# 512-column products, an opening in pieces, column groups in Compressed's first layer and operands at multiples of 512 bytes in a two-block, four-layer kernel

## The chip, the cores and the metric

One core of a Trainium2 chip runs the whole program. The metric is the device time of one execution in microseconds (us), shown as the median of the runs. The engines are PE (TensorE, which multiplies), DVE (VectorE), ACT (ScalarE), POOL (GpSimd) and SP (SyncE, which here issues every DMA).

## The reference, cut to what matters

The input is 256 tokens of width 1024, in float32. Two layers of a first block, then two layers of a second.

```python
# first block, each layer
x = x + 0.5 * (silu(a) * b) @ w2              # a, b = split(rms_norm(x) @ w1), D_FF = 2816
h = rms_norm(x); proj = h @ w_in
ys = gmlp(proj), retention(proj), nsa(proj)   # nsa has the compressed, selected and window branches
x = x + sum(sigmoid(h @ w_gate[b] + bias[b]) * (ys[b] @ w_branch[b]) for b in 3) @ w_o
x = x + 0.5 * swiglu_ffn(rms_norm(x))
# second block, each layer
u = rms_norm(x); proj = u @ w_in
ys = fourier(proj), gqa(proj), mlstm(proj), diff_attention(proj, rel_bias)
x = x + sum(sigmoid(gates[b]) * (ys[b] @ w_branch[b]) for b in 4) @ w_out
x = x + (gelu(conv3(a)) * lin) @ w_down       # a, lin = split(rms_norm(x) @ w_up)
```

Compressed is the branch of nsa that joins windows of 32 tokens into a vector and sends it through a two-layer net (`gelu(flat @ w1) @ w2`).

## The kernel before, in words

**Arithmetic.** Each weight and each activation is split into a high and a low part of type float32r, and a product of matrices is three passes: high by high, high by low, low by high (`three_passes`, L392). In a pass the first operand is stationary (128 x 128) and the second moves through, a column at a time.

**The ring.** All large weights come as 370 tiles of 128 x 2048 values (1 MB). `Ring` (L161) has five slots. For a tile, SP issues the load when the slot is used up (`loads_to`), ACT copies it into its high part (`hi_to`, L198), DVE subtracts to get the low part in place (`lo_to`, L206), and PE waits for that (`ready`). How far ahead each engine works is written out by hand: the calls of `hi_to` and `lo_to` stand between an engine's other work, and each engine runs its list in order.

**Two ways to multiply.** `features_major` (L402) has the weights stationary and hT (the normalised input, features on partitions) moving, 256 tokens wide; `tokens_major` (L413) has hT stationary and 256 weight columns moving. Either takes 48 products of 256 columns for a tile. Down tiles, the output projection and its equal in block two have 512 weight columns moving: 24 products for a tile.

**A feed-forward stage** (`Ffn`, L437) has 11 pairs of up tiles and 11 down tiles. The first pair is done by tokens, so that it can start when the first 128 tokens are normalised, and is turned afterwards (`turn`). Then PE takes up(i, 0), up(i, 1), down(i-1). The up tile fills one PSUM bank with the two halves a and b; ACT applies silu (L567), DVE multiplies by b (L615), ACT and DVE split the result g (L583, L619). In block two a convolution over tokens stands ahead (L572, L607, L610, L577).

**A middle stage** mixes. `Fill` (L670) is a list of units, the halves of projection, gate and branch tiles, which PE works through between the small products of the mixers (`f.tensor(pe, n)`); two PSUM banks take turns. A gate unit ends in a tanh on ACT (L800), a branch unit in one or two DVE operations (L819, L823). `Out` (L834) splits the mixed sum and multiplies it with the output projection.

**Joins.** Between two stages `Join` (L361) adds the result to x, takes the root mean square (ACT L264, POOL L271 to L276), scales (L317, L334), turns on PE (L353) and splits into hT_hi (ACT L325) and hT_lo (DVE L342), for each half of the tokens. PE does products of the first half while the second is being prepared.

**The opening** (`Start`, L2094) does the same for the input, loads the first tiles, and makes the table of relative-position biases: four products give 128 equal rows per head (L2130), DVE copies them (L2139), SP writes them to DRAM and loads them back with a shift of one per partition.

**Compressed** (L1099) has its first layer at L1236: for each of two nets 16 products with the weights stationary and 32 window columns moving.

**Places in SBUF.** Tensors follow each other without gaps, at multiples of 32 bytes. hT and the weight slots have one residue modulo 512 bytes; the overlay with the operands of the stages has others, among them g of the first block, g of the second, and the branch inputs.

```python
pe.matmul(out, w[0], x[0], start=start, stop=False)         # three_passes, L394 to L396
pe.matmul(out, w[0], x[1], start=False, stop=False)
return pe.matmul(out, w[1], x[0], start=False, stop=stop)
```

Of the kernel before, what the change touches and what calls it, by code (L numbers as in the profile page):

```python
# [14 lines left out]
P = 128  # L15
# [22 lines left out]
PROJ1_TILES = 16  # L38
F1_AT = 0
# [6 lines left out]
PROJ2_TILES = 20  # L46
PROJ2_AT = 0
# [76 lines left out]
class Core:  # L124


    def __init__(self, nc, ctx):
# [11 lines left out]
        self.ident = sb("ident", [P, P])  # L139
        self.neg_half = sb("neg_half", [P, 32])  # L140
        self.mean_sq, self.rstd = sb("x_mean_sq", [P, 2, NT, 2]), sb("x_rstd", [P, 2, NT])
# [5 lines left out]
        self.used = [sem(f"w_used{i}") for i in range(SLOTS)]  # L147
        self.res_ok, self.squared, self.rooted, self.xn_dve, self.xn_act, self.turned, self.hT_hi_ok, self.hT_lo_ok = (
# [11 lines left out]

class Ring:  # L161

# [11 lines left out]
    def close(self):  # L174
        self.slot = [n % SLOTS for n in range(len(self.places))]
        self.nth, self.before = [], []
        loads, count = [0] * SLOTS, [0] * SLOTS
        for j, s in zip(self.slot, self.signals):
            loads[j] += 1
            self.nth.append(loads[j])  # L180
            self.before.append(count[j])
            count[j] += s

    def loads_to(self, sp, n):
        for m in range(self.loaded, min(n, len(self.places))):
            slot, at = self.slot[m], self.places[m]
            if self.before[m]:
# [3 lines left out]
            self.loaded = m + 1  # L191

# [168 lines left out]
class Join:  # L361
# [14 lines left out]
    def vector(self, dve):  # L376
        for t in range(NT):
# [45 lines left out]

def ffn_places(base):
# [8 lines left out]
FFN_SIGNALS = [1] * (FFN_TILES - 1) + [2]  # L433
FFN_BYTES = 14336


class Ffn:  # L437
# [3 lines left out]
    def __init__(self, k, ph, r, at, n0, which, norm, conv, res):  # L441
# [6 lines left out]
                                  for j in range(2)] for i in range(2)] for n, a in (("hi", 6144), ("lo", 10240)))  # L448
        self.act_done, self.g_done, self.ghi_done, self.glo_done, self.mid_done, self.conv1, self.conv2 = (
# [7 lines left out]
        self.ab, self.ab0 = k.bank[0:2], k.bank[2:4]  # L457
# [9 lines left out]
    def up(self, pe, i, j):  # L467
# [3 lines left out]
        if i == 1:  # L471
            pe.wait_ge(self.first_ok[j], self.which + 1)
        else:
            pe.wait_ge(self.g_done[j], self.base + i)
        for half in range(2):
            last = features_major(pe, k, slot, half, self.ab[j][:, half * SEQ:(half + 1) * SEQ])
        last.then_inc(k.used[slot], 1)

    def first_up(self, pe, j, t):
        k, n = self.k, self.up_at(0, j)  # L480
        slot = k.ring.slot[n]
        k.ring.ready(pe, n)
        last = tokens_major(pe, k, slot, t, self.ab[j][:, t * 256:(t + 1) * 256],
                            (lambda c: self.norm.ready(pe, t, c)) if j == 0 else None)
# [53 lines left out]
    def scalar(self, act):  # L538
        k = self.k
        for j in range(2):  # L540
            k.ring.wait_used(act, self.up_at(0, j), 1)
            act.activation(self.first[j][:], self.ab[j][:].rearrange("p (t n) -> p t n", t=NT), ACT.Copy
                           ).then_inc(self.first_ok[j], 1)
            k.ring.hi_to(act, self.n0 + SLOTS - 1 + j)
        for j in range(2):
# [3 lines left out]
        for i in range(1, FFN_PAIRS):  # L549
            for j in range(2):  # L550
                self.activate(act, i, j)
                k.ring.hi_to(act, self.up_at(i, j) + SLOTS)
                self.split_hi(act, i, j)
            if i < FFN_PAIRS - 1:
                k.ring.hi_to(act, self.up_at(i, 1) + 1 + SLOTS)

    def activate(self, act, i, j):
        k, at = self.k, self.base + i
        if i:
            k.ring.wait_used(act, self.up_at(i, j), 1)  # L560
        else:
            act.wait_ge(self.first_mm[j], self.which + 1)
        a = self.ab[j] if i else self.ab0[j]
        if self.conv is None:
            if at:
                act.wait_ge(self.g_done[j], at)
            act.activation(self.s1[j][:], a[:, 0:SEQ], ACT.Silu).then_inc(self.act_done[j], 1)  # L567
# [2100 lines left out]
```

## Time and profile before

| | |
|---|---|
| median of 3 runs | 2402.84 us (2400.41 to 2406.5) |
| the profiled execution | 2401.82 us |
| its span, from the first to the last instruction | 2400.1 us |
| mean granted TensorE clock | 0.994 of 2.4 GHz |
| busy: PE, weight loads, DVE, ACT, POOL | 98%, 93%, 58%, 47%, 3% |
| read from HBM | 401.93 MB, 168 GB/s over the span |

The busy share of PE counts overlapping products once, and tells whether it has something to do, not how fast it does it. The distance between the starts of successive products, read from the timeline, tells that. A group of instructions is named by its line, engine and operation, then what it writes and reads (output, arrow, moving operand, stationary operand for PE).

### The profile page before, as it was taken

How to read it: one execution, taken by the hardware profiler on the slowest of the kernel's cores; microseconds unless marked ns; L12 is line 12 of the kernel's file. 1: busy time of each engine (PE TensorE's matmuls, PEld its weight loads, DVE VectorE, ACT ScalarE, POOL GpSimd, SP SyncE). 2: the span in 40 equal slices, each digit the busy share in tenths (PEclk: the TensorE clock that was granted, in tenths of full speed). 3: DMA queues.
4: the chain of work that ended last, by engine and by line, in shares of the span. 5: the costliest groups of instructions: out<-in, count | busy, mean ns of one | idle time of the engine just before them, and what ended most of it. 6: DMA issues, size and time to landing. Idle time of an engine off the chain costs nothing.

```text
span 2400.1 us, 40143 instructions
## 1 busy us (share of the span) xinstructions
PE 2363.1 (98%) x17520; PEld 2233.6 (93%) x17520; DVE 1391.8 (58%) x1730; ACT 1138.0 (47%) x1595; POOL 61.9 (3%) x110
## 2 busy tenths in 40 slices
PE   8999999999999999999999999999999999999998
PEld 7999999999999999999999899999999999999998
DVE  4446656654454466565544655686655655685665
ACT  5435445454354354454543544355545444355543
POOL 0000000000000000000000100000000100000000
PEclk9999999999999999999999999999999999999999
DMA  6564543455555545334555434344555434345553
GB/s 249 181 216 176 198 141 124 158 176 185 184 176 183 214 176 198 129 124 170 209 187 182 158 137 145 135 147 176 185 188 181 159 141 150 131 158 182 178 190 109
DMA packets 60254, 407.13 MB, mean 170 GB/s; under 512 B 7696, under 2 KB 9232, under 8 KB 12464
## 3 DMA queue, kind: packets, MB, share of 16 engines
q1 hardware_dynamic: 60080, 404.58, 47.2%
q8 instruction: 138, 2.26, 0.4%
q14 instruction: 36, 0.29, 0.0%
HBM read 401.93 MB, written 2.10 MB: 168 GB/s over the span
## 4 chain that ended last, share of the span: by engine, by line
PE 89%; DVE 4%; ACT 2%; DMA 2%; issue 1%; POOL 1%; SPq 0%; POOLq 0%; ACTq 0%; DVEq 0%
PE bank L394 27%; PE bank L396 27%; PE bank L395 27%; DVE w_lo L206 2%; DMA w_raw<-in_tiles 2%; DVE hT_lo L342 1%; PE bank L1236 1%; PE bank L1631 1%; PE bank L1458 1%; PE bank L1318 1%; POOL x_rstd L276 1%; PE bank L1855 0%; ACT w_hi L198 0%; ACT a_sq L264 0%; PE bank L1881 0%
## 5 line engine op out<-in xcount | busy, mean ns | idle before, releaser
L394 PE MATMUL bank<-hT_hi,w_hi 128*128 128x256 f32 x3408 | 973.3, 286 | 2.2 <-ACT b_dv L805 1.3
L395 PE MATMUL bank<-hT_lo,w_hi 128*128 128x256 f32 x3408 | 965.6, 283 | 0.0
L396 PE MATMUL bank<-hT_hi,w_lo 128*128 128x256 f32 x3408 | 965.5, 283 | 0.0
L206 DVE TENSOR_TENSOR w_lo<-w_raw,w_hi 128x2048 fp32r<-128x2048 f32 x370 | 843.0, 2285 | 129.9 <-ACT w_hi L198 129.6
L198 ACT ACTIVATE w_hi<-w_raw 128x2048 fp32r<-128x2048 f32 x370 | 705.5, 1909 | 192.2 <-DMA w_raw<-in_tiles 192.0
L394 PEld LDWEIGHTS bank<-hT_hi,w_hi 128*128 128x128 f32 x3408 | 654.3, 192 | 7.5 <-issue 1.9
L395 PEld LDWEIGHTS bank<-hT_lo,w_hi 128*128 128x128 f32 x3408 | 654.5, 192 | 2.6
L396 PEld LDWEIGHTS bank<-hT_hi,w_lo 128*128 128x128 f32 x3408 | 654.3, 192 | 0.0
L615 DVE TENSOR_TENSOR a_ffn_g<-a_ffn_act,bank 128x256 f32<-128x256 f32 x88 | 37.1, 421 | 339.5 <-ACT a_ffn_act L567 339.4
L394 PE MATMUL bank<-w_hi,hT_hi 128*128 128x256 f32 (+1 forms) x736 | 214.9, 292 | 12.3 <-DVE hT_lo L342 9.9
L396 PE MATMUL bank<-w_hi,hT_lo 128*128 128x256 f32 (+1 forms) x736 | 211.6, 287 | 0.0
L395 PE MATMUL bank<-w_lo,hT_hi 128*128 128x256 f32 (+1 forms) x736 | 211.5, 287 | 0.0
L567 ACT ACTIVATE a_ffn_act<-bank 128x256 f32<-128x256 f32 x88 | 33.8, 384 | 295.4 <-PE bank L396 283.9
L394 PEld LDWEIGHTS bank<-w_hi,hT_hi 128*128 128x128 f32 x736 | 145.4, 198 | 19.3 <-issue 10.3
L395 PEld LDWEIGHTS bank<-w_lo,hT_hi 128*128 128x128 f32 x736 | 145.8, 198 | 0.1
L396 PEld LDWEIGHTS bank<-w_hi,hT_lo 128*128 128x128 f32 x736 | 145.6, 198 | 0.0
L394 PE MATMUL bank<-w_hi,a_ffn_g_hi 128*128 128x512 f32 x352 | 140.2, 398 | 0.0
L395 PE MATMUL bank<-w_lo,a_ffn_g_hi 128*128 128x512 f32 x352 | 139.7, 397 | 0.0
L396 PE MATMUL bank<-w_hi,a_ffn_g_lo 128*128 128x512 f32 x352 | 139.7, 397 | 0.0
L607 DVE SCALAR_TENSOR_TENSOR b_ffn_conv<-bank,cols,b_ffn_conv 128x255 f32<-128x255 f32 x44 | 21.2, 482 | 107.1 <-ACT b_ffn_conv L572 107.0
L396 PEld LDWEIGHTS bank<-w_hi,a_ffn_g_lo 128*128 128x128 f32 x352 | 66.5, 189 | 16.2
L394 PEld LDWEIGHTS bank<-w_hi,a_ffn_g_hi 128*128 128x128 f32 x352 | 66.5, 189 | 14.1
(336 smaller groups left out, 2794.6 us busy)
## 6 DMA issues: line engine op xcount, KB each, us to landing
w_raw<-in_tiles SPq DMA_DIRECT2D x370, 1024.0 KB, 4.8
a_cmp_w<-in_cmp_w SPq DMA_DIRECT2D x2, 2048.0 KB, 8.1
a_gm_rows<-in_rows SPq DMA_DIRECT2D x2, 768.0 KB, 6.8
x_res<-in_x SPq DMA_DIRECT2D x2, 512.0 KB, 4.9
rel_line<-a_line SPq DMA_DIRECT2D x1, 1024.0 KB, 8.9
a_ret_rows<-in_rows SPq DMA_DIRECT2D x2, 512.0 KB, 8.4
b_rows<-in_rows SPq DMA_DIRECT2D x2, 512.0 KB, 6.8
out<-x_res SPq DMA_DIRECT2D x4, 256.0 KB, 2.0
```

The lines of the kernel that those rows point to most:

```text
L198: act.activation(k.hi[slot][:], k.raw[slot][:], ACT.Copy).then_inc(k.hi_done[slot], 1)
L206: dve.tensor_tensor(k.lo[slot][:], k.raw[slot][:], k.hi[slot][:].bitcast(F32), ALU.subtract).then_inc(k.lo_done[slot], 1)
L276: pool.tensor_tensor(out, out, k.neg_half[:, 0:1], ALU.pow).then_inc(k.rooted, 1)
L342: dve.scalar_tensor_tensor(out=k.hT_lo[:, c, ts], in0=self.turned(t, c), scalar=self.gain[:, c:c + 1], in1=k.hT_hi[:, c, ts].bitcast(F32), ...
L394: pe.matmul(out, w[0], x[0], start=start, stop=False)
L395: pe.matmul(out, w[0], x[1], start=False, stop=False)
L396: return pe.matmul(out, w[1], x[0], start=False, stop=stop)
L567: act.activation(self.s1[j][:], a[:, 0:SEQ], ACT.Silu).then_inc(self.act_done[j], 1)
L615: dve.tensor_tensor(self.g[j][:], self.s1[j][:], a[:, SEQ:2 * SEQ], ALU.mult).then_inc(self.g_done[j], 1)
L1236: last = pe.matmul(k.bank[i][:, 0:32], self.w1[:, i, j], self.win[i][:, j].rearrange("p g n -> p (g n)"), start=(j == 0), stop=(j == 15))
L1318: last = pe.transpose(k.bank[2 + u % 2][:, j * P:(j + 1) * P], pr[u % 2][:, j * P:(j + 1) * P], k.ident[:])
L1458: last = pe.matmul(self.out_bank[c][:, 0:SEQ], self.m[:, t, c, part * P:(part + 1) * P], self.dft_seq[:, t, part * SEQ:(part + 1) * SEQ], ...
```

## The change

- Up tiles: hT_hi and hT_lo lie next to each other for each group of 128 features. The high weights meet both in one product of 512 columns, the low weights meet hT_hi in one of 256 columns, written over the second half of the bank (`with_both`). A half of an up tile now fills a bank of its own with two partial sums, which ACT (`copy`) and DVE (`add_parts`) add up. The up tiles use four banks in place of two.
- Projections that come out by tokens, and the gates and branches of the second block, move 512 weight columns (`wide`, roles "wide", "wgate", "wbranch"); the weights are laid out on the host to fit (`tile_wide`). The mixed sum of block two is therefore by tokens, and `TurnedOut` turns it on PE ahead of the output projection.
- The first two weight tiles are loaded and split in quarters, and the order of the opening on ACT and DVE is another. The bias table is one product with four rows; the DMA to DRAM repeats them 128 times.
- In Compressed's first layer the windows are stationary and the weights move. Product j goes to the column group j mod 4, that is to 32 of PSUM's partitions; a closing product with four stacked unit matrices adds the groups.
- In a join and at the start of an FFN, weight splits on DVE stand at other places.
- x, hT, the weight slots and the operands of the stages start at multiples of 512 bytes.

The diff, cut to its core:

```diff
+WIDE1 = (0, 6, 8)
+WIDE2 = (0, 10, 12, 18)
...
@@ Core.__init__
+        self.ident = sb("ident", [P, P])
+        self.neg_half = sb("neg_half", [P, 32])
+        self.four, self.four_ok = sb("four", [P, 32]), ctx.enter_context(nc.semaphore("four_ok"))
+        self.mean_sq, self.rstd = sb("x_mean_sq", [P, 2, NT, 2]), sb("x_rstd", [P, 2, NT])
+        sb("up_to_2048", [P, (2048 - nc.sbuf_base) // 32 * 8])
         self.x = sb("x_res", [P, NT, D])
-        self.hT_hi = sb("hT_hi", [P, KC, SEQ], F32R)
-        self.hT_lo = sb("hT_lo", [P, KC, SEQ], F32R)
+        self.hT = sb("hT", [P, KC, 2, SEQ], F32R)
+        self.hT_hi, self.hT_lo = self.hT[:, :, 0], self.hT[:, :, 1]
...
@@ Ring (SPLIT = 2 tiles, PIECES = 4), loads_to and new helpers
+            if m < SPLIT:
+                for q in range(PIECES):
+                    src = self.tiles[at:at + 1, :, q * PIECE:(q + 1) * PIECE]
+                    sp.dma_start(self.piece(self.k.raw, m, q), src.rearrange("a p n -> (a p) n")
+                                 ).then_inc(self.k.piece_in[m][q], 16)
+                self.loaded = m + 1
+                continue
...
+    def piece_hi(self, act, m, q):
+        act.wait_ge(self.k.piece_in[m][q], 16)
+        act.activation(self.piece(self.k.hi, m, q), self.piece(self.k.raw, m, q), ACT.Copy).then_inc(self.k.piece_hi, 1)
...
+    def chunk_ready(self, pe, n, c):
+        if n >= SPLIT:
+            if c == 0:
+                self.ready(pe, n)
+        elif c % 2 == 0:
+            pe.wait_ge(self.k.piece_lo, PIECES * n + c // 2 + 1)
...
@@ Join.vector
                 self.norm.vector_xn(dve, t)
-                self.k.ring.lo_to(dve, self.end + 2 + t)
+                if t == 0:
+                    self.k.ring.lo_to(dve, self.end + 2)
                 self.norm.vector_lo(dve, t)
+        if self.norm is not None:
+            self.k.ring.lo_to(dve, self.end + 3)
...
+def wide(pe, k, slot, t, kh, out, ready=None):
+    ts = slice(t * P, (t + 1) * P)
+    for c in range(KC // 2):
+        at = kh * KC // 2 + c
+        if ready is not None:
+            ready(at)
+        w = slice(c * 512, (c + 1) * 512)
+        last = three_passes(pe, out, (k.hT_hi[:, at, ts], k.hT_lo[:, at, ts]), (k.hi[slot][:, w], k.lo[slot][:, w]),
+                            kh == 0 and c == 0, kh == 1 and c == KC // 2 - 1)
+    return last
+def with_both(pe, k, slot, half, bank):
+    for c in range(KC):
+        at = c * 256 + half * P
+        pe.matmul(bank[:], k.hi[slot][:, at:at + P], k.hT[:, c].rearrange("p a s -> p (a s)"), start=c == 0, stop=False)
+        last = pe.matmul(bank[:, SEQ:2 * SEQ], k.lo[slot][:, at:at + P], k.hT_hi[:, c], start=False, stop=c == KC - 1)
+    return last
...
@@ Ffn.up, from the second pair on
-            pe.wait_ge(self.g_done[j], self.base + i)
+        elif i > 1:
+            pe.wait_ge(self.summed[j], self.parts(i - 1, 1))
         for half in range(2):
-            last = features_major(pe, k, slot, half, self.ab[j][:, half * SEQ:(half + 1) * SEQ])
-        last.then_inc(k.used[slot], 1)
+            with_both(pe, k, slot, half, self.ab[j][half]).then_inc(k.used[slot], 1)
...
@@ Ffn.scalar
         for i in range(1, FFN_PAIRS):
             for j in range(2):
+                self.copy(act, i, j, 0)
+                if not (i == FFN_PAIRS - 1 and j):
+                    k.ring.hi_to(act, self.up_at(i, j) + SLOTS - 1)
                 self.activate(act, i, j)
-                k.ring.hi_to(act, self.up_at(i, j) + SLOTS)
+                self.copy(act, i, j, 1)
                 self.split_hi(act, i, j)
...
+    def copy(self, act, i, j, half):
+        k.ring.wait_used(act, self.up_at(i, j), half + 1)
+        act.activation((self.b if half else self.s1)[j][:], self.ab[j][half][:, SEQ:2 * SEQ], ACT.Copy
+                       ).then_inc(self.copied[j], 1)
...
@@ Ffn.vector (combine's convolution is now a function of its own, convolve)
-        ring.lo_to(dve, self.n0 + SLOTS - 1)
-        for j in range(2):
-            self.combine(dve, 0, j)
         ring.lo_to(dve, self.n0 + SLOTS)
         for j in range(2):
+            self.convolve(dve, 0, j)
+            self.combine(dve, 0, j)
+        for j in range(2):
             self.split_lo(dve, 0, j)
+        ring.lo_to(dve, self.n0 + SLOTS + 1)
         for i in range(1, FFN_PAIRS):
             for j in range(2):
+                self.add_parts(dve, i, j, 0)
+                ring.lo_to(dve, self.up_at(i, j) + SLOTS - 2)
+                self.convolve(dve, i, j)
+                self.add_parts(dve, i, j, 1)
                 self.combine(dve, i, j)
                 self.split_lo(dve, i, j)
+            ring.lo_to(dve, self.up_at(i, 1) + SLOTS - 1)
+    def add_parts(self, dve, i, j, half):
+        out = (self.b if half else self.s1)[j]
+        dve.wait_ge(self.copied[j], self.parts(i, half))
+        dve.tensor_tensor(out[:], self.ab[j][half][:, 0:SEQ], out[:], ALU.add).then_inc(self.summed[j], 1)
...
@@ Fill.product
+        if role[0] in ("wide", "wgate"):
+            ready = (lambda c: self.norm.ready(pe, half, c)) if n <= self.n0 + 1 else None
+            last = wide(pe, k, slot, half, role[-1], bank[:], ready)
...
+        elif role[0] == "wbranch":
+            ts = slice(half * P, (half + 1) * P)
+            for kc in range(YC):
+                w = slice(kc * BW, (kc + 1) * BW)
+                last = three_passes(pe, bank[:], (y_hi[:, kc, ts], y_lo[:, kc, ts]),
+                                    (k.hi[slot][:, w], k.lo[slot][:, w]), kc == 0, kc == YC - 1)
...
+class TurnedOut(Out):
+    def turn(self, pe, half):
+        k, f = self.k, self.f
+        pe.wait_ge(f.mixed, f.mix_at[self.ends[half] - 1])
+        if half:
+            pe.wait_ge(self.mlo_ok, 2)
+        for c in range(KC // 2):
+            for t in range(NT):
+                at, col = (c % 2) * SEQ + t * P, (KC // 2 * half + c) * P
+                last = pe.transpose(k.bank[4 + c // 2][:, at:at + P], f.mix[:, t, col:col + P], k.ident[:])
...
@@ Compressed.tensor
             for j in range(16):
-                last = pe.matmul(k.bank[i][:, 0:32], self.w1[:, i, j], self.win[i][:, j].rearrange("p g n -> p (g n)"),
-                                 start=(j == 0), stop=(j == 15))
-            last.then_inc(self.hid_mm, 1)
-        f.tensor(pe, 2)
+                q = slice(32 * (j % 4), 32 * (j % 4) + 32)
+                last = pe.matmul(k.bank[2 + i][q, 0:P], self.win[i][:, j].rearrange("p g n -> p (g n)"),
+                                 self.w1[:, i, j], start=(j < 4), stop=(j >= 12))
+            last.then_inc(self.part_mm, 1)
+        f.tensor(pe, 1)
+        pe.wait_ge(k.four_ok, 1)
+        for i in range(2):
+            pe.wait_ge(self.part_ok, i + 1)
+            pe.matmul(k.bank[i][:, 0:32], self.parts[i][:], k.four[:], start=True, stop=True).then_inc(self.hid_mm, 1)
+        f.tensor(pe, 1)
...
@@ Start
-        self.line = r.at("line", 39040, [P, DIFF_HEADS, self.W])
+        self.line = r.at("line", 8192, [DIFF_HEADS, self.W])
...
-        k.ring.loads_to(sp, 1)
+        k.ring.loads_to(sp, 2)
...
-        sp.wait_ge(self.copied, DIFF_HEADS)
-        sp.dma_start(line_dram.rearrange("h p n -> p h n"), self.line[:]).then_inc(self.line_out, 16)
+        sp.wait_ge(self.copied, 1)
+        sp.dma_start(line_dram.rearrange("h p n -> h p n"),
+                     self.line[:].unsqueeze(1).broadcast_to([DIFF_HEADS, P, self.W])).then_inc(self.line_out, 16)
...
-        for h in range(DIFF_HEADS):
-            pe.matmul(self.k.bank[4 + h][:], self.rel[:, h:h + 1].broadcast_to([32, P]), self.onehot[:], start=True,
-                      stop=True).then_inc(self.made, 1)
+        pe.matmul(self.k.bank[4][0:DIFF_HEADS, :], self.rel[:], self.onehot[:], start=True, stop=True
+                  ).then_inc(self.made, 1)
...
@@ program: regions of the overlay start at multiples of LINE
+LINE = 512
+        sb("up_to_a_line", [P, -nc.sbuf_base % LINE // 32 * 8])
-        p1.end = 15456
-        r1 = Region(p1, 47424)
+        p1.end = 31 * LINE
+        r1 = Region(p1, 93 * LINE)
-            first.append(Ffn(k, ffn, r1, 24704, a, 2 * l, norm, None, 0.5))
+            first.append(Ffn(k, ffn, r1, 24576, 39424, a, 2 * l, norm, None, 0.5))
+        p2.end = 31 * LINE
+        r2 = Region(p2, 73 * LINE)
...
+def tile_wide(w):
+    N = w.shape[1]
+    return w.reshape(2, KC // 2, P, N // 512, 512).transpose(3, 0, 2, 1, 4).reshape(N // 256, P, TILE)

```

## Rows read from the trace of the kernel before

**Rows 1.** The page: span; busy us, share, count; the chain that ended last, by engine.

```profile
span 2400.1 us, 40143 instructions
PE 2363.1 (98%) x17520; PEld 2233.6 (93%) x17520; DVE 1391.8 (58%) x1730; ACT 1138.0 (47%) x1595; POOL 61.9 (3%) x110
PE 89%; DVE 4%; ACT 2%; DMA 2%; issue 1%; POOL 1%; SPq 0%; POOLq 0%; ACTq 0%; DVEq 0%
```

**Rows 2.** TensorE timeline (start, length, us): up tile, then block-two branch tile.

```profile
106.33 0.28 PE L394 MATMUL bank<-hT_hi,w_hi 128*128 128x256 f32 x1
...
111.72 0.28 PE L394 MATMUL bank<-hT_hi,w_hi 128*128 128x256 f32 x1
...
1543.60 0.28 PE L394 MATMUL bank<-b_z_hi,w_hi 128*128 128x256 f32 x1
...
1546.24 0.28 PE L395 MATMUL bank<-b_z_lo,w_hi 128*128 128x256 f32 x1
```

**Rows 3.** Timeline of TensorE: down tiles of the first block, then of the second.

```profile
100.38 0.40 PE L394 MATMUL bank<-w_hi,a_ffn_g_hi 128*128 128x512 f32 x1
...
105.28 0.40 PE L394 MATMUL bank<-w_hi,a_ffn_g_hi 128*128 128x512 f32 x1
...
1700.69 0.40 PE L394 MATMUL bank<-w_hi,b_ffn_g_hi 128*128 128x512 f32 x1
...
1704.82 0.39 PE L394 MATMUL bank<-w_hi,b_ffn_g_hi 128*128 128x512 f32 x1
```

**Rows 4.** Timeline of TensorE in the opening, at half clock.

```profile
17.62 0.41 PE L395 MATMUL bank<-w_lo,hT_hi 128*128 128x256 f32 x1
17.83 0.41 PE L396 MATMUL bank<-w_hi,hT_lo 128*128 128x256 f32 x1
```

**Rows 5.** Groups by form, TensorE: shapes, count, then busy us, mean ns, idle.

```profile
L394 PE MATMUL bank<-w_hi,a_ffn_g_hi 128*128 128x512 f32 x352 | 140.2, 398 | 0.0
L1236 PE MATMUL bank<-a_cmp_win,a_cmp_w 128*128 128x32 f32 x128 | 14.6, 273 | 0.0
L1258 PE MATMUL bank<-a_cmp_kcT,a_nqT 64*128 64x32 f32 x64 | 4.0, 274 | 0.0
```

**Rows 6.** Groups by form, DVE and ACT.

```profile
L206 DVE TENSOR_TENSOR w_lo<-w_raw,w_hi 128x2048 fp32r<-128x2048 f32 x370 | 843.0, 2285 | 129.9 <-ACT w_hi L198 129.6
L615 DVE TENSOR_TENSOR a_ffn_g<-a_ffn_act,bank 128x256 f32<-128x256 f32 x88 | 37.1, 421 | 339.5 <-ACT a_ffn_act L567 339.4
L567 ACT ACTIVATE a_ffn_act<-bank 128x256 f32<-128x256 f32 x88 | 33.8, 384 | 295.4 <-PE bank L396 283.9 <-PE bank L492 11.3
```

**Rows 7.** Windows: busy us (count) of PE, PEld, DVE, ACT, POOL; PEclk, DMA, GB/s.

```profile
1683.00:1869.00 186.00, 184.18 (x1289) 171.72 (x1288) 113.01 (x133) 95.65 (x116) 0.98 (x3) 1.00 0.53 186
```

**Rows 8.** Timeline of a join, DVE and then TensorE.

```profile
220.61 2.27 DVE L206 TENSOR_TENSOR w_lo<-w_raw,w_hi 128x2048 fp32r<-128x2048 f32 x1
222.81 2.15 DVE L342 SCALAR_TENSOR_TENSOR hT_lo<-bank,cols,hT_hi 128x128 fp32r<-128x128 f32 x8
...
223.20 0.39 PE L394 MATMUL bank<-w_hi,hT_hi 128*128 128x256 f32 x1 [1.15 <-DVE hT_lo L342]
```

**Rows 9.** Timeline of TensorE in the opening.

```profile
6.35 7.19 PE L2130 MATMUL bank<-a_onehot,a_rel 32*128 32x512 f32 x8 [6.35 <-DMA a_onehot<-in_onehot]
...
17.27 0.55 PE L394 MATMUL bank<-w_hi,hT_hi 128*128 128x256 f32 x1 [0.52 <-DVE hT_lo L342]
...
30.86 0.36 PE L394 MATMUL bank<-w_hi,hT_hi 128*128 128x256 f32 x1 [0.54 <-DVE hT_lo L342]
```

**Rows 10.** DMA, first 60 us: GB/s by slice; issues, KB, us to landing.

```profile
GB/s 0 186 301 246 404 391 429 426 421 437 431 404 285 385 437 415 297 22 0 0 0 11 0 109 426 333 431 98 0 197 431 363 233 98 377 235 0 120 426 153
rel_line<-a_line SPq DMA_DIRECT2D x1, 1024.0 KB, 8.9
```

**Rows 11.** Timeline where the first convolution FFN starts, DVE and then TensorE.

```profile
1697.16 2.28 DVE L206 TENSOR_TENSOR w_lo<-w_raw,w_hi 128x2048 fp32r<-128x2048 f32 x1
...
1699.92 0.47 PE L394 MATMUL bank<-w_hi,b_ffn_g_hi 128*128 128x512 f32 x1 [1.23 <-DVE b_ffn_g_lo L619]
```

More of the change, by code:

```diff
@@ L704, in __init__ @@
         for u, (n, h, last, group, role) in enumerate(self.units):
-            if not last and role[0] not in ("gate", "branch"):
+            if self.partial(last, role):
                 continue
-            if role[0] == "branch":
+            if role[0] in ("branch", "wbranch"):
                 counts["mix"] += 1
@@ L718, in __init__ @@
                 counts[key] += 1
[L719 removed]
+                for tile in (n - 1, n) if role[0] == "wide" else (n,):
+                    self.proj_out[tile] = (sems[key], counts[key])
             self.out_of[group] = (sems[key], counts[key])
@@ L723, in __init__, with partial @@
         self.at = {"pe": 0, "act": 0, "dve": 0}
+    @staticmethod
+    def partial(last_half, role):
+        if role[0] in ("wide", "wgate"):
+            return role[-1] == 0
+        return not last_half and role[0] not in ("gate", "branch", "wbranch")
     def bank(self, group):
@@ L801, in activate @@
                            scale=0.5).then_inc(self.gated, 1)
-        elif role[0] != "branch" and last_half and role[3] == "act":
+        elif role[0] == "wgate":
+            b, c, kh = role[1:]
+            if kh:
+                k.ring.wait_used(act, n, half + 1)
+                if b:
+                    act.wait_ge(self.mixed, self.mix_at[self.half_end[b - 1, c] - NT + half])
+                act.activation(self.gate[:, half, c * 512:(c + 1) * 512], self.bank(group)[:], ACT.Tanh, scale=0.5
+                               ).then_inc(self.gated, 1)
+        elif role[0] == "wide":
+            if role[-1]:
+                k.ring.wait_used(act, n, half + 1)
+                func, scale = role[1]
+                out = role[2][:, half]
+                part = self.bank(group)[:] if out.ndim == 2 else self.bank(group)[:].rearrange("p (h b) -> p h b", b=P)
+                act.activation(out, part, func, scale=scale).then_inc(self.act_out, 1)
+        elif role[0] not in ("branch", "wbranch") and last_half and role[3] == "act":
             k.ring.wait_used(act, n, 1)
@@ new lines, in vector @@
+        norm.vector_xn(dve, 0)
+        for q in range(2):
+            ring.piece_lo(dve, 0, q)
+        norm.vector_lo(dve, 0)
+        for q in range(2, PIECES):
+            ring.piece_lo(dve, 0, q)
+        ring.piece_lo(dve, 1, 0)
+        dve.wait_ge(self.made, 1)
+        dve.tensor_copy(self.line[:], k.bank[4][0:DIFF_HEADS, :]).then_inc(self.copied, 1)
+        for q in range(1, PIECES):
+            ring.piece_lo(dve, 1, q)
+        norm.vector_xn(dve, 1)
+        dve.tensor_reduce(k.four[:], k.ident[:].rearrange("p (q n) -> p n q", q=4), AX.X, ALU.add).then_inc(
+            k.four_ok, 1)
```

309 lines of the change are left out of this document (205 added, 104 removed).

## Prediction

> **What bounds the kernel.** I read the page's head first: TensorE is busy for 98% of the span and the chain that ended last is 89% TensorE [rows 1]. A busy TensorE need not run at its peak, so the next view is the timeline of its products, where the distance from one start to the next is the price of a product; the length of one product is longer than that, because products overlap, and isn't used. In an up tile 45 products of 256 columns lie between 106.33 and 111.72 us, 5.39 us: **120 ns each** [rows 2]. In the second block's branch products, whose moving operand lies elsewhere in SBUF, 22 of them take 2.64 us, 120 ns again [rows 2]. The products of 512 columns in the first block's down tiles take 4.90 us for 21, **233 ns**; in the second block's, 4.13 us for 18, **229 ns** [rows 3]. At half clock (1.2 GHz) 256 columns take 0.21 us with nothing on top [rows 4]; so columns alone need 107 and 213 ns at 2.4 GHz, and each product pays some 13 to 20 ns more, whether it has 256 columns or 512. That surcharge is what the change goes for: fewer products for the same columns.
>
> The profiled execution took 2401.8 us with a span of 2400.1, so 1.7 us lie around the span; the median of the runs is 2402.8, 1.0 above it. The sum is made against 2401.8. About 7 us (0.3%) is what a measurement of this kernel can tell from no change.
>
> **Up tiles.** Six FFNs have 20 up tiles after the first pair, each with 16 triples of 256-column products: 1920 triples. hT_hi and hT_lo now lie side by side, so w_hi meets both in one product of 512 columns and w_lo meets hT_hi in one of 256. A triple costs 3 x 120 = 360 ns now and 229 + 120 = 349 after: **-21 us**. I take 229 because two of the trace's kinds of 512-column products have it (Out's too); bounds: 213 (columns alone, -52) and 240 (nothing gained).
>
> **Projections, second gates and second branches.** 14 wide pairs of 96 products (3 per layer in block one, 4 in block two), 32 gate tiles and 16 branch tiles of block two with 48: 3648 products of 256 columns become 1824 of 512, 240 to 229 ns: **-20 us** (bounds -49 and 0).
>
> **Operands at 512 bytes.** hT, the weight slots and the branch operands already had various offsets, and the two offsets of rows 2 cost the same 120 ns, so I book nothing for the 256-column products that stay (4272, and 1920 in the up tiles). For 512 columns the place of the stationary operand does show: 233 against 229 [rows 3]. The first block's 1056 down products (352 in each of three lines [rows 5]) I move to 229: **-4.5 us**. Weights alone hold a product to about 114 ns: 128 products of only 32 columns are busy 14.6 us [rows 5]. That is the lower end for 256 columns, 6 ns on 6192 products (-37 us); the upper end is a few ns the other way.
>
> The Trainium skill's TensorE: Matmul & The Clock Gate, Back-to-back issue gap, gives N/2.4 GHz + 2.5 ns, 109 and 216 ns here. By that rule merging would be worth 2.5 ns on 3744 merged products, 9 us instead of 41. The trace disagrees with it at 120 and 229 ns; the rows decide.
>
> **What the up tiles add.** A sum of two PSUM halves: two copies on ACT and two adds on DVE per tile, 240 each, at 384 and 421 ns [rows 6], so 92 us of ACT and 101 us of DVE. I cost them at nothing: in the window of a convolution FFN (186 us) DVE is busy 113.0 and ACT 95.7 [rows 7]; with 40 adds and copies per FFN they come to 130 and 111. TensorE waits for the second sum only when it returns to the same pair of banks, one up tile and one down tile later (11 us), while copy, add and one weight split in front of it (2.3 us on DVE [rows 6]) take under 5. Behind the added waits stand, on ACT, the next weight's w_hi and the activation; on DVE, w_lo and the convolution; TensorE waits for both, two tiles ahead instead of three. If that cover were gone, each us per up tile would cost 120 us.
>
> **Joins.** At each of nine joins DVE runs a weight split (220.61, 2.27 us) before the second half's hT_lo, which starts at 222.81; TensorE resumes at 223.20 after 1.15 us [rows 8]. The change puts that split behind hT_lo; the next limit is ACT's hT_hi, some 0.7 us earlier: **-6 us**. The split moved is due two tiles later.
>
> **Opening.** Now eight half products of the bias table run at half clock from 6.35 for 7.19 us, the first FFN product starts at 17.27 and the second token half at 30.86 [rows 9]. After: two of the eight half products (6 x 0.9 us less), tiles 0 and 1 in quarters, so splits of a quarter of 2.29 us, the whole tile's [rows 6], stand in front of hT. First product near 9.6; the second half waits for ACT (six quarters, then the second root) until about 18.6: **-12 us** (bounds -8 and -14).
>
> **The bias line.** The same 1 MB is now written from four partitions instead of 128. No row shows a transfer from so few. With 128 it lands in 8.9 us, and 16 engines peak at 437 GB/s, 27 per engine [rows 10]; if the four have the share of one engine, it takes 38 us, if only 4/128 of the total, 77. I take 38, an estimate, because 128 partitions over 16 engines are eight per engine, and four don't fill one. SP has the kept tables (1.3 MB) and tiles 5 to 7 behind it. Issued near 14, it ends at 52; tile 5 lands at 57.5 and is split by 62; TensorE, 12 us ahead of today, wants it near 42: **+20 us** (0 at 8.9, +59 at 77).
>
> The Trainium skill's SBUF — State Buffer, Door 1: The DMA port swizzle, gives 27.6 GB/s for partitions 0 to 3, 38 us here, and the sum by it would be the same 20 us; no run shows it yet, and it speaks against this part of the change.
>
> **Compressed's first layer.** 128 products of 32 columns, 14.6 us busy [rows 5], turn into as many of 128 columns, dealt to four column groups. Products that use half the rows do run two abreast: 64 in 4.0 us, half of 114 ns each [rows 5]. Columns abreast are not shown; bounds 0 and a quarter. I take the quarter, -10.5, less eight closing products at 0.11: **-9.6 us**.
>
> **Second Out.** mix is now by tokens and is turned on TensorE: 32 transposes at 0.11 us: **+3.5 us**; waits for them lie behind a branch unit of 2.75 us (12 x 229 ns).
>
> **Convolution start.** A weight split at 1697.16 stands before g_lo, and TensorE waits 1.23 us at 1699.92 [rows 11]; the change puts it behind: **-2.5 us** for the two layers and the tail of the first.
>
> Sum: -21 - 20 - 4.5 - 6 - 12 + 20 - 9.6 + 3.5 - 2.5 = -52. 2401.8 - 52 = **2350 us**, and with the median's distance still 2350 to 2351.
>
> **Rivals.** *Equal offsets free the products* (0.28): with both operands at multiples of 512 bytes, weight reads stop delaying the columns, 512-column products fall to 216, just over what their columns need, and 256 to 114. 5712 x 13 + 6192 x 6 = 74 + 37 us less: **2239**, or 2276 if only the former fall. For it: 233 against 229 shows that place counts. Against: hT and weights had the same residue already, and 120 ns stayed. By the formula of the Trainium skill's TensorE: Matmul & The Clock Gate named above, 216 and 109, the time would be 2208.
>
> *The line lands quickly* (0.10): no stall in the first FFN: **2330**.
>
> *Equal offsets collide* (0.08, the slow side): all 5712 products of 512 columns now have moving and stationary operand on one residue, which no 512-column row has. Each ns costs 5.7 us; from 238 ns on the whole gain is gone; at 242: **2424**. Against: two other residues differ by only 4.
>
> *The column groups do not run abreast* (0.07): that part of the change does not do what it says, +10.5: **2360**.
>
> The forecast itself has 0.47, spread 2325 to 2385 by the bounds of the line and of 229. The range 2235 to 2388 leaves out the lower edge of the first rival and the slow side, together under 0.2. Faster by over 0.3%: 0.90, the four cases below 2395 less the forecast's upper edge; within: 0.03; slower: 0.07, most of the slow side.
>
> **What would show it.** In the changed trace: starts of an up tile's triple 349 ns apart in sum, wide products 229; no weight split between xn and hT_lo at a join, and its stall under 0.5 us; the first FFN product near 9.6 and the second half near 18.6 us; rel_line landing after some 38 us and a TensorE wait for w_lo of about 20 us near 45; 32 Compressed products in under 1 us. I am wrong if 512-column products leave 225 to 235 ns, if 256-column ones leave 120, or if TensorE waits for DVE in the FFNs.

## The result and the profile after

The changed kernel takes **2387.08 us** (2383.74 to 2388.02, 4 runs) against 2403.03 for the kernel before in the same comparison: ratio 0.9928, 95% interval 0.991 to 0.9945. It is 16 us faster where 52 were forecast. The time lies inside the range, the direction was right, the size was wrong by 37 us.

First the page of the changed kernel: span, busy time, and the chain that ended last.

```profile
span 2384.9 us, 33194 instructions
PE 2313.0 (97%) x13810; PEld 2020.8 (85%) x13810; DVE 1500.2 (63%) x1978; ACT 1219.3 (51%) x1817; POOL 62.8 (3%) x110
PE 89%; DVE 3%; ACT 3%; DMA 1%; SPq 1%; issue 1%; POOL 0%; DVEq 0%; POOLq 0%; ACTq 0%
```

Against [rows 1], PE has 3710 products less, 50 us less busy time, and *more* idle time: 72 us of the span in place of 37. So cheaper products are there, and a wait has come with them. Where it lies shows a table of stages, each counted from the first transpose at one join to the first at the next, the last one to the start of TensorE's last product (from the two timelines of TensorE, in us):

| stage | before | after | difference |
|---|---|---|---|
| up to the opening's first transpose | 14.80 | 7.63 | -7.2 |
| first FFN of layer 1 | 197.98 | 226.97 | +29.0 |
| middle stages of block one | 269.97, 269.93 | 259.90, 260.19 | -10.1, -9.7 |
| the other three FFNs of block one | 192.22, 192.06, 195.35 | 189.26, 189.18, 192.45 | -3.0, -2.9, -2.9 |
| middle stages of block two | 337.70, 334.60 | 331.43, 328.26 | -6.3, -6.3 |
| convolution FFNs | 194.00, 194.07 | 196.18, 196.10 | +2.2, +2.0 |

Three stages got slower. In the first FFN, TensorE stands still once, for 32 us; the timeline of TensorE (the bracket: idle time, and who ended it), then SP's queue (start and length of an issue):

```profile
70.84 0.77 PE L438 MATMUL bank<-w_hi,a_ffn_g_hi 128*128 128x512 f32 x1 [32.46 <-DVE a_ffn_g_lo L720]
```

```profile
15.20 0.81 SPq L2358 DMA_DIRECT2D rel_line<-a_line  x1
16.05 14.54 SPq L2361 DMA_DIRECT2D a_decay<-in_decay  x1
...
43.41 12.76 SPq L208 DMA_DIRECT2D w_raw<-in_tiles  x3
59.86 1.76 SPq L2366 DMA_DIRECT2D shifted<-rel_line  x4
```

ACT, once tile 4 was copied, had nothing to do until tile 5 landed, nor had DVE behind it: ACT's list has the copy of tile 5 ahead of the first activation. So TensorE waits for the g_lo that this activation leads to, and not for tile 5 itself. The timeline of ACT:

```profile
26.84 1.91 ACT L239 ACTIVATE w_hi<-w_raw 128x2048 fp32r<-128x2048 f32 x1
65.73 1.91 ACT L239 ACTIVATE w_hi<-w_raw 128x2048 fp32r<-128x2048 f32 x1 [36.98 <-DMA w_raw<-in_tiles]
```

The bias line is issued at 15.20. SP is done with its other issues at 56.17 and waits for the line until 59.86, so the 1 MB takes some 45 us. In a view of the transfers of 20 to 30 us the rate settles at 25 GB/s with 2 tenths of the 16 engines busy; in the kernel before, 1 MB landed in 8.9 us [rows 10]. Behind it SP needs 14.54 us to issue *one* transfer of 768 KB (0.51 in the kernel before): the queue itself is held up, which the prediction had not priced.

```profile
DMA  6865553222125222222122221222122221222122
GB/s 295 369 270 229 238 205 98 74 49 33 16 25 98 25 25 25 25 25 33 16 25 33 25 33 16 25 25 33 16 33 25 25 33 16 25 25 33 16 33 25
```

The products themselves, in an up tile and in a down tile of the first block:

```profile
99.69 0.40 PE L485 MATMUL bank<-hT,w_hi 128*128 128x512 f32 x1
99.93 0.28 PE L486 MATMUL bank<-hT,w_lo 128*128 128x256 f32 x1
...
100.75 0.40 PE L485 MATMUL bank<-hT,w_hi 128*128 128x512 f32 x1
...
228.00 0.39 PE L439 MATMUL bank<-w_lo,a_ffn_g_hi 128*128 128x512 f32 x1
...
233.66 0.39 PE L440 MATMUL bank<-w_hi,a_ffn_g_lo 128*128 128x512 f32 x1
```

A triple costs 1.06/3 = **353 ns** (360 before, 349 forecast). The 25 down products from 228.00 to 233.66 cost 5.66/25 = **226 ns** (233 in [rows 3]). Over all down products of block one that run at full clock without a wait, the mean falls by less, from 233.7 to 229.5 ns.

At a convolution FFN's start the wait has moved, not gone (DVE's list, then TensorE):

```profile
1696.81 0.42 DVE L720 TENSOR_TENSOR b_ffn_g_lo<-b_ffn_g,b_ffn_g_hi 128x256 fp32r<-128x256 f32 x1 [0.48 <-ACT b_ffn_g_hi L670]
1697.16 2.29 DVE L247 TENSOR_TENSOR w_lo<-w_raw,w_hi 128x2048 fp32r<-128x2048 f32 x1
1699.50 0.50 PE L485 MATMUL bank<-hT,w_hi 128*128 128x512 f32 x1 [3.35 <-DVE w_lo L247]
```

g_lo of the first down tile is in time, and the 1.23 us of [rows 11] are gone. But now a split of a weight tile stands *behind* all the work of the up pair, and TensorE waits 3.35 us for it. At the joins the second half's wait is shorter, and a new one stands in front of the first half's transposes (TensorE):

```profile
234.60 1.06 PE L394 MATMUL bank<-ident,a_xn 128*128 128x128 f32 x8 [0.55 <-DVE a_xn L375]
...
244.22 0.50 PE L438 MATMUL bank<-w_hi,hT 128*128 128x512 f32 x1 [0.44 <-DVE hT L383]
```

### The profile page after: what moved, and what is told of

Read it like the earlier page. It is cut to its first block, busy times and chain, and to the rows that moved or that the text cites. A ratio compares the mean times of both kernels' runs of the same rounds, so it can differ in the third digit from the quotient of the medians.

```text
span 2384.9 us, 33194 instructions
## 1 busy us (share of the span) xinstructions
PE 2313.0 (97%) x13810; PEld 2020.8 (85%) x13810; DVE 1500.2 (63%) x1978; ACT 1219.3 (51%) x1817; POOL 62.8 (3%) x110
## 4 chain that ended last, share of the span: by engine, by line
PE 89%; DVE 3%; ACT 3%; DMA 1%; SPq 1%; issue 1%; POOL 0%; DVEq 0%; POOLq 0%; ACTq 0%
PE bank L438 18%; PE bank L440 18%; PE bank L439 18%; PE bank L485 18%; PE bank L486 9%; DMA w_raw<-in_tiles 1%; ACT w_hi L239 1%; SPq L2361 1%; DVE w_lo L247 1%; PE bank L1871 1%; PE bank L1698 1%; PE bank L1558 1%; PE bank L2095 0%; PE bank L394 0%; PE bank L2121 0%
## 5 line engine op out<-in xcount | busy, mean ns | idle before, releaser
L485 PE MATMUL bank<-hT,w_hi 128*128 128x512 f32 x1920 | 684.4, 400 | 6.7 <-DVE w_lo L247 6.7
L486 PE MATMUL bank<-hT,w_lo 128*128 128x256 f32 x1920 | 540.8, 282 | 0.0
L485 PEld LDWEIGHTS bank<-hT,w_hi 128*128 128x128 f32 x1920 | 362.7, 189 | 96.1 <-DVE w_lo L247 7.3
L486 PEld LDWEIGHTS bank<-hT,w_lo 128*128 128x128 f32 x1920 | 364.7, 190 | 2.0
L438 PE MATMUL bank<-hT,w_hi 128*128 128x256 f32 x976 | 282.8, 290 | 0.0
L438 PE MATMUL bank<-w_hi,hT 128*128 128x512 f32 (+2 forms) x768 | 274.3, 357 | 8.2 <-DVE hT L383 5.5
L439 PE MATMUL bank<-hT,w_hi 128*128 128x256 f32 x976 | 277.4, 284 | 0.0
L440 PE MATMUL bank<-hT,w_lo 128*128 128x256 f32 x976 | 277.3, 284 | 0.0
L440 PE MATMUL bank<-w_hi,hT 128*128 128x512 f32 (+2 forms) x768 | 269.1, 350 | 0.0
L439 PE MATMUL bank<-w_lo,hT 128*128 128x512 f32 (+2 forms) x768 | 269.1, 350 | 0.0
L438 PEld LDWEIGHTS bank<-hT,w_hi 128*128 128x128 f32 x976 | 188.4, 193 | 1.4 <-ACT a_gate L938 0.7
L439 PEld LDWEIGHTS bank<-hT,w_hi 128*128 128x128 f32 x976 | 188.7, 193 | 0.3
L440 PEld LDWEIGHTS bank<-hT,w_lo 128*128 128x128 f32 x976 | 188.4, 193 | 0.0
L438 PEld LDWEIGHTS bank<-w_hi,hT 128*128 128x128 f32 x768 | 146.5, 191 | 34.2 <-issue 9.4
L440 PEld LDWEIGHTS bank<-w_hi,hT 128*128 128x128 f32 x768 | 146.4, 191 | 19.5
L439 PEld LDWEIGHTS bank<-w_lo,hT 128*128 128x128 f32 x768 | 146.7, 191 | 17.9
L694 DVE TENSOR_TENSOR a_ffn_act<-bank,a_ffn_act 128x256 f32<-128x256 f32 x80 | 33.9, 424 | 174.6 <-ACT a_ffn_act L644 174.6
```

The lines of the kernel that those rows point to most:

```text
L485: pe.matmul(bank[:], k.hi[slot][:, at:at + P], k.hT[:, c].rearrange("p a s -> p (a s)"), start=c == 0, stop=False)
L486: last = pe.matmul(bank[:, SEQ:2 * SEQ], k.lo[slot][:, at:at + P], k.hT_hi[:, c], start=False, stop=c == KC - 1)
L694: dve.tensor_tensor(out[:], self.ab[j][half][:, 0:SEQ], out[:], ALU.add).then_inc(self.summed[j], 1)
```

## The experiments

The edits are shown cut to their core, some of them in words.

**The bias line from 128 partitions.**

```diff
-pe.matmul(bank[4][0:DIFF_HEADS, :], rel, onehot)
+dve.tensor_copy(rel128, rel, each head 32 times)
+pe.matmul(bank[4], rel128, onehot)
-line [4, W], each row written 128 times
+line [128, W], each row written 4 times
```

> The changed kernel, but the bias table is made as 128 rows (each head 32 times) and the 1 MB is written from 128 partitions, four times each, instead of from four. Theory (the transfer from four partitions, some 25 GB/s, holds back tile 5): the TensorE stall of 32.6 us at 38.1 us falls to under 3 us, the time to 2354 to 2358 us. Rival (tile 5 would be late anyway, because TensorE is ahead by 11 us and the kept tables stand in front): the stall stays over 10 us, 2365 or more.

Measured: **2351.68 us**, ratio 0.9794 (0.9778 to 0.9811), 35.4 us less than the changed kernel and a little below the theory's range. SP's queue and the transfer's landing (the last number, us):

```profile
15.58 0.63 SPq L2359 DMA_DIRECT2D rel_line<-a_line  x1
16.25 0.62 SPq L2362 DMA_DIRECT2D a_decay<-in_decay  x1
rel_line<-a_line SPq DMA_DIRECT2D x1, 1024.0 KB, 9.8
```

The issue behind the line takes 0.62 us instead of 14.54, the stall is gone altogether. The theory holds; the few partitions cost 35 us. The run takes away the long transfer and the hold-up of SP together, so it doesn't say how much either costs.

**One row per head.** The loads need no copies at all if they read overlapping windows of one row.

```diff
-line written 128 times; load at [[W - 1, 128], [1, SPAN]]
+line copied backwards, written once; load at [[1, 128], [1, SPAN]]
-bias read at [[-128, 2], [1, SEQ]]
+bias read at [[128, 2], [-1, SEQ]]
```

> The changed kernel, but only one row per head (8 KB in all) is written, backwards; the shifted loads read overlapping windows of it, and the second block reads the shifted table backwards. Theory (the 1 MB is the whole trouble): no stall at tile 5, 2352 to 2357 us, a little under the kernel with 128 partitions. Rival (the shifted loads or the kept tables delay it): over 2365.

Measured: **2349.28 us**, ratio 0.9782 (0.9767 to 0.9796). A little better than the former, as expected, though below the range given. It is the base of most runs below.

**The same four rows, from partitions 0, 32, 64 and 96.**

```diff
-self.line[:].unsqueeze(1).broadcast_to([4, 128, W])
+self.line[::32].unsqueeze(1).broadcast_to([4, 128, W])
```

> The changed kernel; the bias line is again written by one transfer from four partitions, 128 times each, but from partitions 0, 32, 64 and 96 in place of 0 to 3. If the neighbourhood of the four partitions (one port) limits the transfer: four times faster, some 11 us, no long stall, 2353 to 2358 us. If a transfer whose rows lie in four partitions uses four engines, or one partition gives 6 GB/s: still 25 GB/s and some 42 us, the stall over 28 us, 2384 to 2390.

Measured: 2365.12 us in one run, TensorE's wait 13.54 us: between the two answers. SP's queue:

```profile
15.41 0.67 SPq L2359 DMA_DIRECT2D rel_line<-a_line  x1
16.14 9.17 SPq L2362 DMA_DIRECT2D a_decay<-in_decay  x1
...
40.38 2.25 SPq L2367 DMA_DIRECT2D shifted<-rel_line  x4
```

SP's last wait for the line ends at 40.38, so it took some 25 us, 42 GB/s in the mean. In a view of the transfers of 20 to 40 us the rate falls to 49 GB/s where little else runs:

```profile
GB/s 356 229 188 111 98 78 115 66 53 49 49 86 172 180 311 381 267 215 230 74 49 98 152 299 49 53 139 116 53 49 156 143 143 381 340 401 365 361 332 340
```

That the four partitions are neighbours costs a factor of two, 25 against 49 GB/s, and not the four of the first answer; that they are only four still costs 13 us of waiting. Why it is two, no run here shows.

**Up tiles without the 512-column product.**

```diff
-pe.matmul(bank[:], hi, hT[:, c]) ; pe.matmul(bank[:, 256:512], lo, hT_hi[:, c])
+8 x pe.matmul(bank[:, 0:256], hi, hT_hi[:, c])
+8 x (pe.matmul(bank[:, 256:512], hi, hT_lo[:, c]) ; pe.matmul(bank[:, 256:512], lo, hT_hi[:, c]))
```

> The changed kernel, but in up tiles the product of 512 columns is undone: hi x hi, then hi x lo and lo x hi, 256 columns each, into the same two halves of the bank, so that ACT's copies and DVE's adds stay. Theory from the trace after (a triple costs 353 ns merged, 360 apart): +13 us, 2400. The prediction's price (349): +21, 2408. Rival (TensorE waits for DVE and ACT in the FFNs, so that the price of a triple does not count): under +4.

Measured: 2396.07 us, ratio 0.9978 (0.9969 to 0.9988): **+9.0** to the changed kernel. In three of block one's FFNs the stage is 2.0 us longer, which 320 triples at 6 to 7 ns give; in the convolution FFNs only 1.6 and 0.6. Merging is worth 9, not 21, and not quite the 13 of the theory either.

**Triples in another order.**

```diff
 FFN 1: the 256-column product goes to bank[:, 0:256]
 FFN 2: from the second group on, 256 columns ahead of 512
 FFN 3: eight products of 512 columns, then eight of 256
```

> The kernel with one bias row per head; the up tiles' triples differ by FFN, so the trace is read, not the time. FFN 0, 4, 5: as changed (353 ns). FFN 1: the 256-column product is added to the first half of the bank. FFN 2: from the second group on, the 256-column product goes ahead of the 512-column one. FFN 3: the eight of 512 columns first, then the eight of 256. Theory (the 9 ns over 227 belong to the change of size behind it): FFN 3 near 347 a triple, FFN 1 and 2 at 353. Rival (they belong to the half of the bank written twice): FFN 1 at 347. Rival (they belong to the operands): 353 in all.

One run; the prices are read from the timeline of TensorE, here a tile of FFN 3 (xN: so many products run together in a row):

```profile
1171.32 1.12 PE L489 MATMUL bank<-hT,w_lo 128*128 128x256 f32 x8
1172.27 2.00 PE L485 MATMUL bank<-hT,w_hi 128*128 128x512 f32 x8
1174.11 0.64 PE L489 MATMUL bank<-hT,w_lo 128*128 128x256 f32 x4
```

Eight of 256 columns take 0.95 us from start to start, eight of 512 take 1.84: 119 + 230 = **349 ns** a triple. In FFN 1 the triple stays at 353, so the half of the bank isn't it. But FFN 2, which alternates as well, costs 350, and in a stretch of it five triples take 1.73 us, 346 each:

```profile
701.23 0.40 PE L485 MATMUL bank<-hT,w_hi 128*128 128x512 f32 x1
...
702.96 0.39 PE L485 MATMUL bank<-hT,w_hi 128*128 128x512 f32 x1
```

So the order of the products decides on some 4 ns of a triple, but that the alternation of sizes costs them is not shown: the theory asked for 353 in FFN 2. What in the order does it stays open.

**Wide products halved.**

```diff
-three products of 512 columns per group of features
+each as two of 256 columns, but for the first and last of an accumulation
```

> The kernel with one bias row per head (2349.3 us), and 1320 of the 1440 products of 512 columns in the wide projections and second gates halved again. Theory from the trace (227 ns against twice 120): 13 ns each, +17 us, 2366. The prediction's price (229): +14.5, 2364. Rival (the middle stages wait for the mixers' small work, not for these products): under +8.

Measured: 2368.62 us (2365.05 to 2370.87): **+19.3**, or +15.2 in the profiled runs (2365.05 against 2349.88), 12 to 15 ns for each of 1320. This part is worth what the trace after says, slightly more than the 11 forecast.

**The changed kernel without its pads.**

```diff
-sb("up_to_2048", ...)
-sb("up_to_a_line", ...)
```

> The changed kernel without the two pads: x, hT and the weight slots start 448 bytes, the operands of the stages 352 bytes behind a multiple of 512. Theory (the place of an operand sets 2 to 6 ns of a 512-column product, 227 against 229 to 233): +11 to +34 us, 2398 to 2421. Rival (the place does nothing, the 227 has another reason): within 4 us of 2387. A third way (the 256-column products leave 120 ns as well): over +40.

Measured: 2393.90 us, ratio 0.9969 (0.9956 to 0.9981): +6.8, less than the theory's lower end. Down products:

```profile
227.71 0.39 PE L437 MATMUL bank<-w_hi,a_ffn_g_hi 128*128 128x512 f32 x1
...
229.81 0.39 PE L437 MATMUL bank<-w_hi,a_ffn_g_hi 128*128 128x512 f32 x1
```

Nine products in 2.10 us, **233 ns**, and 226 in the changed kernel. But wide products, whose two operands (weights and hT) share the residue 448 here, stay at 227 (median of their starts in the trace), and the alternating triple is 2 to 3 ns *cheaper* in the mean (350.5). Two effects of opposite sign, so the sum is small.

**The kernel before, with pads alone.**

```diff
+sb("up_to_1536", ...) ahead of x; the overlay at a multiple of 512
+p1.end = 30 * 512 + 384    (g of block one at a multiple of 512)
+p2.end up to a multiple of 512    (g of block two too)
```

> The kernel before with pads alone: x, hT, the weight slots and g of the first block's FFNs start at multiples of 512 bytes, nothing else changed. Theory (a product of 512 columns costs 227 ns when both operands have one residue, a product of 256 stays at 120): 1056 products 6 ns cheaper, -6 us, 2396. Rival (multiples of 512 free all products): 256 columns under 118 ns, below 2380. Rival (the place does nothing): 2402.

Measured: 2393.57 us against 2402.94, ratio 0.9963 (0.995 to 0.9976): -9.4, some 3 more than the 1056 products explain. The pads move more than the expectation says: all operands of the stages get other places. Down products of the first block:

```profile
100.23 0.39 PE L397 MATMUL bank<-w_hi,a_ffn_g_lo 128*128 128x512 f32 x1
...
102.29 0.39 PE L397 MATMUL bank<-w_hi,a_ffn_g_lo 128*128 128x512 f32 x1
```

Nine in 2.06 us, 229 here and 227 in the median of all, where [rows 3] had 233. Products of 256 columns with hT stay at 120. But the 576 branch products of block one, 256 columns too, get cheaper; the first and last of 96 in a row, in the kernel before and then in this one:

```profile
450.39 0.28 PE L394 MATMUL bank<-a_y_hi,w_hi 128*128 128x256 f32 x1
...
461.79 0.28 PE L396 MATMUL bank<-a_y_hi,w_lo 128*128 128x256 f32 x1
```

```profile
448.11 0.29 PE L395 MATMUL bank<-a_y_hi,w_hi 128*128 128x256 f32 x1
...
458.90 0.28 PE L397 MATMUL bank<-a_y_hi,w_lo 128*128 128x256 f32 x1
```

11.40/95 = **120 ns** before, 10.79/95 = **114 ns** here. By the sizes in the code these operands, too, had the weights' residue modulo 512 before; here they lie at 192 and the weights at 0. So the place counts for 256 columns as well, the other way about, and 576 products at 5 to 6 ns are the 3 us. In the kernel without pads (352 against 448) they cost 118. In this kernel, the changed one and the one without pads, a 512-column product is cheapest (227) where moving and stationary operand have one residue, be it 0 or 448.

**Two weight tiles moved in ACT's and DVE's lists** (on one row per head).

```diff
 ACT:  hi_to(up_at(i, j) + 4)  ->  + 4 + (i == 1 and j == 0), and not left out at the FFN's last up tile
 DVE:  lo_to(up_at(i, j) + 3)  ->  + 3 + (i == 1 and j == 1)
```

> The kernel with one bias row per head (2349.3 us), and two weight tiles moved in the lists of ACT and DVE: in the first pair after the start of each FFN tile 6 is copied and split one place earlier; at the end of an FFN ACT copies the next stage's first tile in front of the last activation. Theory (these stalls are the order of DVE's list: 3.5 us twice at a convolution FFN's start, 2.2 and four times 0.7 us in front of the joins): -8 to -12 us, 2337 to 2341. Rival (DVE and ACT are simply full there, so that the wait moves to the next tile): within 3 us of 2349.

Measured: **2339.30 us**, ratio 0.973 (0.9709 to 0.9751), -10.0. DVE's list where TensorE had waited 3.35 us:

```profile
1657.02 0.42 DVE L693 TENSOR_TENSOR b_ffn_act<-bank,b_ffn_act 128x256 f32<-128x256 f32 x1
1657.36 2.28 DVE L247 TENSOR_TENSOR w_lo<-w_raw,w_hi 128x2048 fp32r<-128x2048 f32 x1
1659.56 0.48 DVE L701 SCALAR_TENSOR_TENSOR b_ffn_conv<-b_ffn_act,cols,b_ffn_conv 128x255 f32<-128x255 f32 x1
```

The split now stands ahead of the second convolution, in time in which DVE had waited for ACT. The engines were not full; the order was wrong by one place.

**The split at the joins put back** (on the former).

```diff
-if t == 0: lo_to(end + 2)  ...  after both halves: lo_to(end + 3)
+lo_to(end + 2 + t) ahead of each half's hT_lo
```

> The kernel of 2339.3 us, and the weight split at the joins put back in front of the second half's hT_lo on DVE. The prediction's price: +6 us, 2345. By the stalls in front of the second half's first product (1.05 to 1.47 us before, 0.6 to 0.7 after): +4 to +6. Rival (the transposes of the first half are the later wait, so the second half's does not count): under +2.

Measured: 2343.79 us, ratio 0.9749 (0.973 to 0.9767): **+4.5**. TensorE's wait in front of the second half is 1.31 us again:

```profile
209.53 0.50 PE L435 MATMUL bank<-w_hi,hT 128*128 128x512 f32 x1 [1.31 <-DVE hT L383]
```

**Up tiles with the sizes grouped** (on the kernel of 2339.3).

```diff
 for c: pe.matmul(bank[:], hi, hT[:, c])
+for c:
     pe.matmul(bank[:, 256:512], lo, hT_hi[:, c])
```

> The kernel of 2339.3 us (one bias row per head, the weight tiles moved), and in every up tile the eight products of 512 columns first, then the eight of 256. Theory from the run with different triples (the alternation of sizes costs 4 to 6 ns a triple; 1920 triples): -8 to -11 us, 2328 to 2332. Rival (a tile that needs its low weights later only moves the wait): within 3 us of 2339.

Measured: **2329.57 us**, ratio 0.969 (0.9671 to 0.9709), -9.7. A triple costs 349 ns in the median of all. The kernel beats both others, by 73.5 and 57.5 us; PE is busy for 99% of the span.

```profile
span 2327.9 us, 33194 instructions
PE 2298.2 (99%) x13810; PEld 2018.9 (87%) x13810; DVE 1499.1 (64%) x1978; ACT 1219.7 (52%) x1817; POOL 62.7 (3%) x110
```

## Why the prediction was right in sign and wrong in size

Step by step, forecast and found, in us:

| step | forecast | found | shown by |
|---|---|---|---|
| bias line from four partitions | +20 | +35 | run with 128 partitions: 35.4 less |
| up tiles | -21 | -9 to -13 | run unmerged; 353 against 360 ns |
| convolution start, ends of FFNs | -2.5 | +7.5 | run with tiles moved: 10.0 less, taken off the -2.5 |
| joins | -6 | -4.5 | run with the split put back |
| opening | -12 | -10.5 | second half's first product at 20.31, 30.86 in [rows 9] |
| projections, gates, branches | -20 | -22 to -27 | run halved: 12 to 15 ns on 1320, taken for all 1824 |
| down products, Out | -4.5 | -5 to -8 | means of all; 227 against 233 and 229 |
| Compressed | -9.6 | -9.2 | 14.6 to 4.3 us, below, and 1.1 for the eight closing products |
| transposes of the second Out | +3.5 | +4 | below |

The groups of TensorE for the last two (count, busy us, mean ns):

```profile
L1471 PE MATMUL bank<-a_cmp_w,a_cmp_win 128*32 128x128 f32 x128 | 4.3, 276 | 0.0
L1078 PE MATMUL bank<-ident,b_mix 128*128 128x128 f32 x32 | 4.1, 272 | 0.0
```

**The bias line** is the largest miss, 15 of 37 us. The mechanism was right: four partitions carry the line slowly, and tile 5 comes behind it ("it ends at 52; tile 5 lands at 57.5 and is split by 62"). The term was mis-sized in three places. First, the line was priced at 38 us and took some 45: it ended near 59.9, and tile 5 was copied at 65.73, again some 6 us behind it. That is 8 us more. The Trainium skill's SBUF — State Buffer, Door 1: The DMA port swizzle, gives 27.6 GB/s for partitions 0 to 3, near the 25 GB/s of the trace. Second, "wants it near 42" had the path wrong. The copy of tile 5 stands ahead of the first activation in ACT's list, so TensorE stood still from 38.1 on, for g_lo: 4 us more. Third, the granted clock fell during the long wait, and some ten products behind it ran at half clock: 2 us more (below). The 14.54 us for which SP was held weren't priced at all; since tile 5 was taken to land behind the line anyway, no run shows that they add to this.

**Up tiles.** The step that failed is "229 + 120 = 349 after", with 229 "because two of the trace's kinds of 512-column products have it". Those rows were of products that follow their like. In an up tile 512 and 256 columns take turns, and the pair costs 353. The nearest row was the wrong one; the kernel with sizes grouped gives 349 and another 10 us. What in the order makes the 4 ns stays open, as FFN 2 of the run with triples in another order shows.

**"I cost them at nothing", the added copies and sums.** For the bulk of an FFN that holds: no wait for a sum of over 0.3 us stands in the changed kernel's up tiles. At the edges it failed. The prediction named what stands behind the added waits (w_hi, w_lo, "two tiles ahead instead of three"), but checked the sum of busy time and the wait for banks, not the first pair and the last, where a queue has no lead. There the order of DVE's list cost 10 us, and -2.5 had been booked.

**Rivals.** "Equal offsets free the products" is wrong: 256 columns stay at 120, 512 at 227, where it asked for 114 and 216. What does reach 114 is 256 columns at unequal residues, in the kernel before with pads. The formula of the Trainium skill's TensorE: Matmul & The Clock Gate, Back-to-back issue gap, gives 216 and 109, for a product by itself, and is 11 ns below either here. "Equal offsets collide" is wrong the other way for its 512 columns: equal residues are the cheapest found. "The line lands quickly" is wrong in this kernel, and its 2330 is what the improved one reaches by other ways. The column groups do run abreast.

Adding what was missed (line 15, up tiles 8 to 12, edges of the FFNs 10, joins and opening 3) and taking off what came better (wide products 2 to 7, down products up to 4) gives 25 to 38 us, around the 37. The single terms are no closer known than that.

## What to carry to other kernels

When a step is moved to fewer partitions, price the transfer and the queue behind it first: here 1 MB by the wrong route cost more than all the merged products of the up tiles gained. The price of a product is read from a row with the same neighbours and the same places, not only the same shape. And an added operation that is free by busy time is not free at a stage's first and last tile; walk those two in each engine's list.

## What was not expected of the hardware

- A transfer from four neighbouring partitions ran at 25 GB/s, and the issue of the next one took 14.54 us. From four partitions 32 apart it ran at 49 GB/s, and the next issue took 9.17 us.
- A 512-column product costs 227 ns with both operands at the same residue modulo 512 bytes and mostly 229 to 238 otherwise. A 256-column product costs 120 ns at the same residue and, in block one's branches, 114 to 118 otherwise. So the place that is cheapest for one is the dearest found for the other; no kernel here makes use of that for the 256-column products with hT.
- 512 and 256 columns in turn cost 353 ns a pair in the changed kernel, grouped 349, and in turn with the 256 first 350.
- In the stretches that begin where waits of 32.46 and of 3.35 us end, TensorE's mean granted clock was 0.53 and 0.62: part of them ran at half clock (1.2 GHz). Without the first wait the same stretch was at full clock (2.4 GHz). The windows of the changed kernel (us, then busy time of PE, PEld, DVE, ACT, POOL with counts, PEclk, DMA share, GB/s):

```profile
38.10:70.84 32.74, 0.28 (x2) 0.03 (x1) 1.32 (x4) 4.87 (x7) 0.00 (x0) 0.55 0.61 177
70.84:76.00 5.16, 5.16 (x13) 4.10 (x14) 3.83 (x6) 1.39 (x6) 0.00 (x0) 0.53 0.17 68
1699.50:1704.00 4.50, 4.50 (x17) 3.83 (x18) 3.71 (x5) 2.33 (x4) 0.00 (x0) 0.62 0.18 76
```

and of the kernel with the line from 128 partitions:

```profile
70.84:76.00 5.16, 5.16 (x27) 4.32 (x26) 4.39 (x5) 3.83 (x5) 0.00 (x0) 1.00 0.49 176
```

In the same 5.16 us TensorE did 27 products in place of 13. The wait of 3.35 us cost some 1.7 us more in this way (0.38 of 4.50 us).
